# Expert weights of a diffusion trunk step loaded in 4 KB packets in place of 16 KB and 8 KB

## The reference

```python
def _expert_choice(h, router, w1, w3, w2):
    ...
    cap = EC_FACTOR * (bsz * n_tok) // N_EXPERTS
    aff = jax.nn.softmax((xf @ router).astype(jnp.float32), axis=-1)
    gate, idx = lax.top_k(aff.T, cap)
    xe = xf[idx]
    he = jax.nn.silu(jnp.einsum('ecd,edf->ecf', xe, w1)) * jnp.einsum('ecd,edf->ecf', xe, w3)
    ye = jnp.einsum('ecf,efd->ecd', he, w2) * gate[..., None].astype(h.dtype)
    y = jnp.zeros_like(xf).at[idx.reshape(-1)].add(ye.reshape(-1, dm))
    ...
```

## Time and profile before

| what | value |
|---|---|
| median of 3 runs | 2893.16 us (2885.23 to 2896.66) |
| profiled execution, its own time | 2892.97 us |
| profiled execution, span | 2891.2 us |
| mean granted clock of PE | 0.945 |
| PE busy | 2492.4 us, 86% |
| DVE, ACT, POOL busy | 42%, 19%, 21% |
| DMA | 76605 packets, 560.85 MB, mean 194 GB/s |

### The profile page before, as it was taken

How to read it: one execution, slowest core, us unless ns; L and a number is a source line. 1 busy time by engine, 2 the same in 40 slices (tenths; PEclk the granted TensorE clock), 3 DMA queues, 4 the chain that set the end, 5 groups by cost and what they waited for, 6 DMA issues and landing times. The chain is left out here.

```text
span 2891.2 us, 76516 instructions
## 1 busy us (share of the span) xinstructions
PE 2492.4 (86%) x34482; PEld 1738.0 (60%) x34482; DVE 1200.2 (42%) x2514; ACT 550.5 (19%) x1174; POOL 614.4 (21%) x754
## 2 busy tenths in 40 slices
PE   6999989798866999999779999887988479999994
PEld 3576545596445666666346765556863366666662
DVE  3477846545342121111254877564453411111213
ACT  2111533221110010000131134332221101000101
POOL 1254500233130000000142535003221300000002
PEclk9999999999978999999899999999999689999997
DMA  7011000104646999999730011001145379999994
GB/s 291 8 43 39 14 30 1 64 26 179 247 161 229 396 400 393 393 398 408 278 142 25 26 41 41 1 1 64 49 189 228 146 284 395 394 396 392 398 387 162
DMA packets 76605, 560.85 MB, mean 194 GB/s; under 512 B 14024, under 2 KB 15880, under 8 KB 37368
## 3 DMA queue, kind: packets, MB, share of 16 engines
q1 hardware_dynamic: 70136, 534.97, 46.6%
q0 software_dynamic: 6144, 20.98, 3.1%
HBM read 528.78 MB, written 27.13 MB: 192 GB/s over the span
## 5 line engine op out<-in xcount | busy, mean ns | idle before, releaser
L2661 PE MATMUL ps<-arena 128*64 128x80 f32 x16384 | 614.0, 235 | 63.4 <-issue 58.7
L2661 PEld LDWEIGHTS ps<-arena 128*64 128x64 f32 x16384 | 587.6, 138 | 111.2 <-issue 108.5
L2757 DVE TENSOR_TENSOR arena<-arena,ps 128x160 f32<-128x160 f32 x128 | 41.2, 322 | 651.6 <-ACT arena L2710 651.6
L2675 PE MATMUL ps<-arena 128*64 128x512 f32 x1024 | 256.1, 610 | 10.4 <-issue 5.3
L2710 ACT ACTIVATE arena<-ps 128x160 f32<-128x160 f32 x128 | 38.9, 304 | 847.3 <-PE ps L2661 847.3
L735 PE MATMUL ps<-arena,x_sb 128*128 128x512 f32 (+1 forms) x704 | 194.7, 435 | 3.5 <-ACT arena L924 1.9
L2418 POOL DMA_INDIRECT sum_d<-arena x32 | 45.6, 1426 | 648.3 <-DVEq L2750 648.3
L735 PEld LDWEIGHTS ps<-arena,x_sb 128*128 128x128 f32 x704 | 107.9, 191 | 89.3 <-issue 84.2
L1859 POOL TENSOR_TENSOR arena<-arena,rwl_sb 128x512 f32<-128x512 f32 x50 | 64.1, 1289 | 413.8 <-ACT arena L1801 344.3
L2679 PE MATMUL ps<-arena 128*16 128x256 f32 x2048 | 136.4, 382 | 0.0
L2412 POOL DMA_INDIRECT arena<-h_d,arena x32 | 40.3, 1258 | 419.9 <-DVEq L2728 352.2
(11 more groups left out here) (361 smaller groups left out, 3982.1 us busy)
## 6 DMA issues: line engine op xcount, KB each, us to landing
arena<-in_ex_w SPq DMA_DIRECT2D x128, 2048.0 KB, 16.2
arena<-in_ex_w SPq DMA_DIRECT2D x128, 1024.0 KB
arena<-in_ada_w SPq DMA_DIRECT2D x32, 1024.0 KB, 6.9
arena<-in_ada_w SPq DMA_DIRECT2D x8, 2048.0 KB, 21.1
x_sb<-in_w_t SPq DMA_DIRECT2D x22, 512.0 KB, 4.2
arena<-in_w_t SPq DMA_DIRECT2D x12, 512.0 KB, 6.6
x_sb<-in_x SPq DMA_DIRECT2D x2, 2560.0 KB, 16.1
h_d<-x_sb SPq DMA_DIRECT2D x10, 512.0 KB, 2.6
```

Source lines behind the costliest of these rows:

```text
L2661: m = nc.tensor.matmul(gated(j)[c * 64:(c + 1) * 64, f, a, :], w13[q % WG][:, a, k, f * P + c * 64:f * P + (c + 1) * 64], xT[:, x % 2, k, ...
L2675: nc.tensor.matmul(sample_out(x, h), he[:, x % 2, f, 0:CAPS], w2[:, q % WP, f % 2, h * 512:(h + 1) * 512], start=f == 0, stop=f == KD - 1)
```

## The change

The weights lie in memory in another order, and a load names its slot in rows of 4 KB. A w13 load becomes 4 blocks (w1 or w3, times two halves of k) of 128 partitions x 4 KB, 512 packets; a w2 load becomes 2 blocks (f) of 128 partitions x 4 KB, 256 packets. The number of transfers, their bytes, slots, order, semaphores and what lies where in a slot are as before.

```diff
@@ layout
-        "ex_w13": np.stack([f("ex_w1"), f("ex_w3")], 2).reshape(DEPTH, NE, 2, KD, P, 4, 256).transpose(0, 1, 5, 4, 2, 3, 6),
-        "ex_w2": f("ex_w2").reshape(DEPTH, NE, 4, 2, P, DM).transpose(0, 1, 2, 4, 3, 5),
+        "ex_w13": np.stack([f("ex_w1"), f("ex_w3")], 2).reshape(DEPTH, NE, 2, 2, KD // 2, P, 4, 256).transpose(0, 1, 6, 2, 3, 5, 4, 7),
+        "ex_w2": f("ex_w2").reshape(DEPTH, NE, 4, 2, P, DM),
@@ load_w13
-    sp.dma_start(mem["w13"][q % WG].rearrange("p a k n -> p (a k n)"), e.d["ex_w13"][e.l, q // 4, q % 4].rearrange("p a k n -> p (a k n)")
+    sp.dma_start(mem["w13"][q % WG].rearrange("p a (h k) n -> p (a h) (k n)", h=2), e.d["ex_w13"][e.l, q // 4, q % 4].rearrange("a h p k n -> p (a h) (k n)")
@@ load_w2
-    sp.dma_start(mem["w2"][:, q % WP].rearrange("p f n -> p (f n)"), e.d["ex_w2"][e.l, q // 4, q % 4].rearrange("p f n -> p (f n)")
+    sp.dma_start(mem["w2"][:, q % WP], e.d["ex_w2"][e.l, q // 4, q % 4].rearrange("f p n -> p f n")
```

## The result

The changed kernel takes 2910.32 us (median of 5 runs, 2906.15 to 2917.32) against 2893.16 us before (median of 5, 2880.8 to 2896.66). The ratio is 1.0066, with a 95% interval from 1.0046 to 1.0085: 0.66% slower, some 19 us, where 42 us (1.5%) were forecast. The profiled execution took 2917.32 us, the slowest of the five, so its rows show some 7 us more than the median.

The account below looks back on a forecast made before the run. PE was taken to set the pace of the expert phases, with DMA nearly at its limit. Layer 0's 22.3 us plus layer 1's 19.8 (22.3 less 2.5 cover) gave 42.1, so 2935 us, 1.5% slower; range 2880 to 2980.

Parts of the forecast that it names:

- What bounds the kernel: Expert phases: PE sets the pace, but the DMA queue is always full, falls behind and ends just in time.
- The cover: Layer 1's expert phase: w2 slots loaded ahead hide the first 0.7 to 4.7 us of lag, taken as 2.5.
- nothing hides the lag in layer 0: Layer 0's expert phase: no cover left, since L2675 already waits 4.0 us; the full 22.3 us counts.
- The place of the waits: PE waits for in_ex_w at L2675 rather than L2661, some 20 us a layer, over each phase's second half.
- The speed of 4 KB packets by themselves: Weight loads: 4 KB packets alone move at 406 GB/s, against 429 for 16 KB and 423 for 8 KB.
- The slow stretches of 388 and 363 GB/s: Two of three loads of x in the new w13 layout; at these speeds +43 or +76 us a layer.
- the sum's only term: Expert phases: 184.5 MB of weights a layer at 406 GB/s, 454 us against 432.1, +22.3 us before cover.
- the forecast's own range: Whole kernel: 2908 to 2958 us, for speeds of some 395 to 415 GB/s, +15 to +65 us; chance 0.50.
- Rival 3: Expert phases: small packets mix better with other traffic, "issue" gaps shrink; 19 us a layer faster, 2855 us; chance 0.10.
- Rival 1: Packets hardly matter (421 GB/s), 1 MiB transfers get full bandwidth: +6.1 and +3.6 us, 2903 us; chance 0.20.
- The fixed cost of about 3 cycles for each packet: Weight loads: four 4 KB packets cost 524 cycles against 515 for one of 16 KB; +6.6 us a layer.
- SP was held up: Issuing more packets holds SP, at most 25.6 us in the output and 15.4 in the route phase; costed at nothing.

Follow-up runs that it names:

- half_16k: Kernel before with half of PE's gate work left out (4 of 8 blocks of rows summed), loads whole; 2867.93 us.
- w2_4k: Kernel before with only the w2 loads in 4 KB packets, w13 unchanged; 2899.33 us, ratio 1.0028.
- w13_4k_pad: Kernel before with only w13 loads in 4 KB packets, a partition's rows one behind the other in memory, each padded by 256 bytes; 2906.41 us, ratio 1.0046.
- half_4k: Changed kernel with the same half of PE's gate work left out as in half_16k; 2885.63 us.
- The eight kernels: half_16k, half_4k and their twins without adds, without most gathers, or without both; 2755.54 to 2867.93 us with 16 KB, 2790.91 to 2885.63 with 4 KB.
- w13_8k: Kernel before with the w13 loads in 8 KB packets, two for each of 16 KB, w2 as before; 2890.43 us, ratio 0.9990.
- all_2k: Changed kernel with both w13 and w2 loads in 2 KB packets; 2962.66 us, ratio 1.0244 to the kernel before.

## Why the prediction was right and wrong

**What bounds the kernel** was read rightly. The page's waits named PE, the DMA side was nonetheless close to its limit, and the growing time from issue to landing gave it away. half_16k shows it by experiment: with PE's gate work halved, the speed went from 396 to 400 GB/s.

**The cover** was right in kind: w2_4k made PE wait in layer 0 and not in layer 1. Its size, 2.5 us, is not shown: in the changed kernel layer 1 lost 4.3 us less than layer 0, and two profiles of the kernel before differ by as much in such a comparison. That nothing hides the lag in layer 0 went too far. The 4.0 us wait of before stands at 1414.66 us, near the phase's end, and in the changed kernel L2675 first waits there after 1100 us, some 200 us into the phase.

**The place of the waits** was L2675 in both layers, and nothing moved at L2661. The forecast had some 20 us a layer, the trace has 26.5 and 17.2. But that is not the loss, since part of it took the place of "issue" gaps.

**The speed of 4 KB packets by themselves**, 406 GB/s, was right, with some luck. It was the middle of four stretches from 363 to 421, and its own stretch was not of 4 KB packets alone, though the prediction says so: 78 of its 673 are under 512 B. But the five preloads of layer 1, which ran at 429 GB/s before, now show

```profile
DMA packets 2029, 8.07 MB, mean 404 GB/s; under 512 B 62, under 2 KB 62, under 8 KB 2027
```

The slow stretches of 388 and 363 GB/s were no measure of the layout, which w13_4k_pad shows to cost nothing. What slowed them stays open.

**The step that failed is the sum's only term, 22.3 us a layer.** It took the difference of two speeds measured alone (432.1 us of weight time against 454) and added it to a phase in which the engines also serve the software queue, as if the friction between them stayed as it was. half_16k against half_4k measures the same term under load: 8.9 us a layer. With it the sum is 8.9 + 8.9 - 2.5 = 15 us, against 19 by the ratio, whose interval (13 to 25 us) holds it. The sum gave 42. The measured 2910 us still lies at the lower edge of the forecast's own range (2908 to 2958), because that range also took in speeds near the best stretch. The eight kernels say where the other half went: without gathers the term is 16.5 to 17.7 us a layer, with gathers it is 8.4 to 8.9. So half of the term comes back at the gathers, because a gather costs more beside large packets. Leaving out 28 of them saved 54.7 us with 16 KB packets (2867.93 to 2813.18) and 39.4 us with 4 KB (2885.63 to 2846.20). Of the 22.3 us, some 5 were also too much by themselves: with an empty software queue 423 became 408 GB/s, 3.5% and not the 5% from 427 to 406.

**Rival 3** was right in one of its two halves: small packets do mix better, and the "issue" gaps did shrink by 15.4 us. But the saving is with the gathers alone, not with the adds, and is half as large as the cost of the packets. The gaps give nothing back as long as the DMA side is the slower one; w13_8k repeats this with 43.1 us of gaps and the time of before.

**Rival 1**, by its number, came nearer than the sum: 2903 us, 7 below the measured time, where 2935 is 25 above it. Its reason is ruled out by w13_4k_pad and all_2k: the transfer's size is the same in all of them, and the time rises with the packets. The fixed cost of about 3 cycles for each packet, which the prediction took from the Trainium skill (DMA: Bandwidth & Descriptors, "Why small descriptors are slow (HBM only)"), gave an estimate of 6.6 us a layer. That is nearer to the loaded 8.9 us than the sum was, but for the wrong reason: with the queue to themselves the packets lose 17.7 us.

**SP was held up**, as said, and it cost nothing that shows. In layer 0 the five preloads took it 12.28 us (2.98 before), and the first store of h2 behind them was issued at 786.22, 1.5 us later than before, as the preloads themselves were. In the expert phase the DMA share stayed at 1.02, so the engines never ran out of work. The lines are the five preloads of layer 1, 2.30 us before, and a w13 and a w2 issue in the expert phase, 0.33 us before:

```profile
2215.66 10.70 SPq L2429 DMA_DIRECT2D arena<-in_ex_w  x5
...
2747.05 3.31 SPq L2429 DMA_DIRECT2D arena<-in_ex_w  x1
...
2750.40 7.16 SPq L2435 DMA_DIRECT2D arena<-in_ex_w  x1
```

Still open is what happens inside a DMA engine when a gather's packets meet 16 KB packets; only its price was measured. Open too is why the step from 4 to 2 KB, with the gathers in place, costs more for each packet than the step to 4 KB.

## What to carry to other kernels

An engine that never waits for data may still be carried by slots loaded ahead: look at how the time from issue to landing grows over the phase before calling the transfers hidden. When DMA is at its limit, keep rows long on both sides, 8 KB or more here; the cost came with more packets (not in proportion), not with where the rows lie in memory. And a difference of speeds measured alone is not a difference under load: here the loaded one was half as large. So price a change of packet size with the other queues' traffic in place.

## What the hardware showed that was not expected

- In the kernels with half of the gate work, gathers of 80 rows of 4 KB cost 2.0 us each (54.7 / 28) beside 16 KB packets and 1.4 us beside 4 KB packets, though 0.33 MB at the 423 GB/s of the free queue would be 0.8 us. Adds of the same size cost 1.6 us (52 / 32) beside either; 44 of the 52 us lie within the expert phases.
- 16 KB and 8 KB packets for w13 cannot be told apart in time (0.9990), 4 KB for w13 cost 0.47%. Going from 4 to 2 KB for all weights costs 1.8%.
- With smaller packets the gaps of PE that no semaphore explains shrank from 58.7 to 43.3 us. They do so where w13 alone is in packets of 4 KB (43.8 us) or 8 KB (43.1 us), and not where w2 alone is (58.0 us).
